# Feed-forward down projection as one level of Strassen's scheme, with one weight sum of each step made by GpSimd

## The reference, cut to what matters

```
D_MODEL = 1024; SEQ = 512; DEPTH = 4; D_FF = 2816

def conv_ffn(x, w_up, conv_w, conv_b, w_down):
    h = x @ w_up                                   # 512 x 1024 times 1024 x 5632
    h = causal_depthwise_conv(h, conv_w) + conv_b  # width 3, each channel by itself
    gate, val = jnp.split(h, 2, axis=-1)
    return (jax.nn.silu(gate) * val) @ w_down      # 512 x 2816 times 2816 x 1024

for i in range(DEPTH):
    ...
    x = x + rms_norm(m, post_mix)
    x = x + rms_norm(conv_ffn(rms_norm(x, pre_ffn), *ffns[i]), post_ffn)
```

## Time and profile before

| | us |
|---|---|
| runs of the kernel before (3) | 2116.58, 2116.76, 2118.89; median 2116.76 |
| profiled execution: span from first to last instruction | 2114.8 |
| profiled execution: another time than its span | none given by the page |
| TensorE matmuls busy, x11988 | 2104.0 |
| DVE busy | 1178.3 |
| ACT busy | 918.0 |
| GpSimd busy | 166.3 |
| HBM traffic | 211.63 MB, mean 100 GB/s |

### The profile page before, as it was taken

The page is one execution under the profiler, slowest core; times in us unless marked ns, Lnnn a source line. Parts: engine busy times, 40 slices in busy tenths (PEclk is TensorE's granted clock), DMA queues, the critical chain, the costliest instruction groups (busy, mean ns, idle before and its releaser), DMA issues.

```text
span 2114.8 us, 32799 instructions
## 1 busy us (share of the span) xinstructions
PE 2104.0 (99%) x11988; PEld 1774.6 (84%) x11988; DVE 1178.3 (56%) x1918; ACT 918.0 (43%) x1527; POOL 166.3 (8%) x190
## 2 busy tenths in 40 slices
PE   9999999999999999999999999999999999999998
PEld 8889888888989888888877898888889889888887
DVE  6665555536366555544697665555446665555534
ACT  5754333325335433333556553334344754333423
POOL 1510000000000000000046300000000520000000
PEclk9999999999999999999999999999999999999999
DMA  7224233331431323333321123333342132333331
GB/s 281 71 90 130 90 98 99 109 136 53 140 130 51 105 94 99 99 109 129 110 77 40 60 77 99 99 99 99 100 139 100 62 101 70 99 99 99 100 99 60
DMA packets 60365, 211.63 MB, mean 100 GB/s; under 512 B 6720, under 2 KB 10944, under 8 KB 59888
## 3 DMA queue, kind: packets, MB, share of 16 engines
q1 hardware_dynamic: 52416, 190.03, 27.4%
q10 hardware_dynamic: 7856, 20.34, 2.7%
HBM read 208.19 MB, written 6.34 MB: 101 GB/s over the span
## 4 chain that ended last, share of the span: by engine, by line
PE 98%; DVE 1%; DMA 0%; ACT 0%; issue 0%; SPq 0%; DVEq 0%; ACTq 0%
PE ps L1545 24%; PE ps L1473 17%; PE ps L1475 17%; PE ps L1474 17%; PE ps L1656 6%; PE ps L1501 2%; PE ps L1503 2%; PE ps L1502 2%; PE ps L1519 1%; PE ps L1518 1%; PE ps L1517 1%; PE ps L1533 1%; PE ps L1819 1%; PE ps L1727 1%; PE ps L1778 1%; PE ps L1701 1%
## 5 line engine op out<-in xcount | busy, mean ns | idle before, releaser
L1473 PE MATMUL ps<-h_hi,w_hi 128*128 128x512 f32 (+1 forms) x1552 | 606.6, 391 | 0.0
L1474 PE MATMUL ps<-h_lo,w_hi 128*128 128x512 f32 (+1 forms) x1552 | 603.2, 389 | 0.0
L1475 PE MATMUL ps<-h_hi,w_lo 128*128 128x512 f32 (+1 forms) x1552 | 603.2, 389 | 0.0
L1427 DVE SCALAR_TENSOR_TENSOR work<-ps,conv_sb,work 128x511 f32<-128x511 f32 (+1 forms) x352 | 247.4, 744 | 437.4 <-ACT work L967 437.1
L1031 DVE TENSOR_TENSOR w_lo<-raw,w_hi 128x1024 fp32r<-128x1024 f32 x312 | 385.8, 1241 | 52.8 <-ACT w_hi L606 43.0
L967 ACT ACTIVATE work<-ps,conv_sb 128x512 f32<-128x512 f32 x176 | 137.2, 779 | 515.2 <-PE ps L1475 486.0
L606 ACT ACTIVATE w_hi<-raw 128x1024 fp32r<-128x1024 f32 x324 | 337.9, 1048 | 34.3 <-PE ps L1545 14.2
L1473 PEld LDWEIGHTS ps<-h_hi,w_hi 128*128 128x128 f32 x1552 | 291.4, 188 | 62.9 <-issue 4.0
L1475 PEld LDWEIGHTS ps<-h_hi,w_lo 128*128 128x128 f32 x1552 | 291.3, 188 | 60.2
L1474 PEld LDWEIGHTS ps<-h_lo,w_hi 128*128 128x128 f32 x1552 | 291.5, 188 | 58.6
L1545 PE MATMUL ps<-w_hi,a_hi 128*128 128x512 f32 x608 | 187.2, 389 | 0.0
(11 more groups left out here) (211 smaller groups left out, 2632.1 us busy)
## 6 DMA issues: line engine op xcount, KB each, us to landing
raw<-slabs SPq DMA_DIRECT2D x324, 512.0 KB, 3.8
bias<-slabs SPq DMA_DIRECT2D x28, 512.0 KB, 6.2
bias_dram<-bias_rows ACTq DMA_DIRECT2D x2, 2048.0 KB, 13.3
g_post<-gains ACTq DMA_DIRECT2D x8, 512.0 KB, 4.2
bias<-bias_dram ACTq DMA_DIRECT2D x2, 2048.0 KB, 9.7
g_pre<-gains ACTq DMA_DIRECT2D x7, 512.0 KB, 5.3
x<-x_in SPq DMA_DIRECT2D x4, 512.0 KB, 7.6
bias<-bias_dram SPq DMA_DIRECT2D x1, 2048.0 KB, 7.7
```

Source lines behind the costliest of these rows:

```text
L1427: ve.scalar_tensor_tensor(y, ps[:, 2 * par + e, 0:SEQ - sh], conv_sb[:, L, t, tap:tap + 1], y, ALU.mult, ALU.add).then_inc(done, 1)
L1473: pe.matmul(ps[:, bank, cols], hi, h_hi[:, k, cols], start=k == 0, stop=False)
L1474: pe.matmul(ps[:, bank, cols], hi, h_lo[:, k, cols], start=False, stop=False)
L1475: last = pe.matmul(ps[:, bank, cols], lo, h_hi[:, k, cols], start=False, stop=k == KT - 1)
```

## The change

One level of Strassen's scheme (Winograd's form) takes the place of the 4 x 2 blocks. Two slabs make a step: the activations of the two slabs, split by token halves, are A11, A12, A21, A22, the slabs' column halves are B11, B12 (even slab) and B21, B22 (odd slab). Seven half products take the place of eight, each for two token tiles of 128 and 512 columns, three matmuls each. All seven are summed over the 11 steps in PSUM before they are combined.

- **Activations, GpSimd** (`down_sums`): five instructions of 256 columns a step (three sums or differences, a copy, another difference), beside the up projection as soon as both gate products of a step are there.
- **Weights, four sums of 512 columns a step**: T1 = B12-B11 on GpSimd (`t1_sum`); T3 = B12-B22 (`sums`), T2 = B11-T3 (`next_sum`), B21-T2 (`last_sum`) on DVE, in place in `raw`. `next_sum` overwrites B12, so it waits for T1. For steps 3 on, T1 is written over activations whose remainder is made, so it waits for `op_lo` of its step.
- **First phase** (P1, P6, P7, P4): 24 matmuls a step, 22 slabs through the ring.
- **Second phase** (P5): 6 matmuls a step, with T1 split into half a ring slot.
- **Third phase** (P2, P3): 12 matmuls a step; the odd slabs are loaded a second time. Tile 0 of the last four steps is done before tile 1.
- DVE combines the products: P1-P7 (`third`), plus P6, plus P4 (`c21`); then P5's sum plus P1 (`c12`), and `c22`. P2 and P3 go on top of what lies in the banks.
- Token tiles 0 and 1 are complete before the third phase, so their norms stand inside it. The early slabs are loaded into `act`, after T1's remainders are made, and split behind the third phase.
- The operand ring: 1024-wide operands for steps in `a_hi`, `h_hi` and their remainders.

The core of the diff (waits on constants and unchanged helpers are left out):

```diff
+            def t1_sum(L, j):
+                even = DOWN[L] + 2 * j
+                b11, b12 = raw[:, raw_slot(even), 0:SEQ], raw[:, raw_slot(even), SEQ:D]
+                pool.wait_ge(raw_in[raw_slot(even)], raw_count(even))
+                if j >= 2:
+                    pool.wait_ge(op_lo, STEPS * L + (j + 1 if j > 2 else 1))
+                pool.tensor_tensor(t1_place(j), b12, b11, ALU.subtract).then_inc(t1_made, 1)
+
+            def down_sums(L):
+                for j in range(STEPS):
+                    if j == STEPS - 1:
+                        for c in range(3):
+                            t1_sum(L, c)
+                    a21, a11, a22, a12 = quarters(j)
+                    s1, kept, s4 = s1_place(j), pa_place(j)[:, 0:HALF], pa_place(j)[:, HALF:SEQ]
+                    pool.wait_ge(gated, FFT * L + 2 * j + 2)
...
+                    pool.tensor_tensor(s1, a21, a22, ALU.add).then_inc(s_made, 1)
+                    pool.tensor_copy(kept, a12).then_inc(s_made, 1)
+                    pool.tensor_tensor(a21, a11, a21, ALU.subtract).then_inc(s_made, 1)
...
+                    pool.tensor_tensor(a12, s1, a11, ALU.subtract).then_inc(s_made, 1)
...
+                    pool.tensor_tensor(s4, kept, a12, ALU.subtract).then_inc(s_made, 1)
+                for j in range(3, STEPS):
+                    t1_sum(L, j)
```

DVE, in the up projection's last pairs and in the down projection:

```diff
+                pair(0, FFT // 2 - 2)
+                pair(1, FFT // 2 - 2)
+                sums(L, 0)
+                next_sum(L, 0)
+                last_sum(L, 0)
                 pair(0, FFT // 2 - 1)
+                sums(L, 1)
+                operand(L, 0)
+                next_sum(L, 1)
+                last_sum(L, 1)
                 pair(1, FFT // 2 - 1)
+                sums(L, 2)
...
+                operand(L, 1)
+                next_sum(L, 2)
+                operand(L, 2)
+                last_sum(L, 2)
+                operand(L, 3)
+                for j in range(3, STEPS):
+                    split_lo(n0 + 2 * j - 2)
+                    sums(L, j)
+                    split_lo(n0 + 2 * j - 1)
+                    next_sum(L, j)
+                    if j + 1 < STEPS:
+                        operand(L, j + 1)
+                    last_sum(L, j)
+                split_lo(n0 + FFT - 2)
+                split_lo(n0 + FFT - 1)
+                t1(0), t1(1), third(0), third(1), t1(2), t1(3), c21(0), c21(1)
+                for j in range(4, STEPS):
+                    t1(j)
+                second(0), second(1), c12(0), c12(1), c22(0), c22(1), second(2), second(3)
+                y(0), add(0), second(4), norm(0), y(1), second(5), add(1), second(6), norm(1)
+                for j in range(7, STEPS):
+                    second(j)
+                lo(0), lo(1), split_early(n), y(2), add(2), split_early(n + 1), norm(2)
+                split_early(n + 2), y(3), add(3), split_early(n + 3), lo(2), norm(3), lo(3)
```

(the calls of one line stand one below the other in the kernel; without the pre-norm the last layer leaves out `norm`, `lo` and the early slabs.) TensorE:

```diff
+                for j in range(1, STEPS - 1):
+                    arrived(j)
+                    p1(j, 0)
+                    p1(j, 1)
+                    p6(j, 0)
+                    p6(j, 1).then_inc(w_used, 1)
+                    odd_arrived(j)
+                    p7(j, 0)
+                    p7(j, 1)
+                    p4(j, 0)
+                    p4(j, 1).then_inc(w_used, 1)
```

```diff
+                ring_slabs(n1 + EARLY, DOWN[L] + FFT)
+                for j in range(STEPS):
+                    if j == RAW and L + 1 < DEPTH:
+                        early_slabs(n2)
+                    ring(second_slot(L, j))
```

More of the change, by code:

```diff
@@ L272, in made, with raw_slot, raw_count, dram @@
         def made(c):
-            return c + 1 - EARLY * passed(c)
+            return c + 1 - EARLY * passed(c) - STEPS * sum(n + FFT + STEPS <= c for n in DOWN)
+        def raw_slot(c):
+            return (made(c) - 1) % RAW
+        def raw_count(c):
+            return 16 * ((made(c) - 1) // RAW + 1)
+        def dram(c):
+            L = max(i for i in range(DEPTH) if BASE[i] <= c)
+            c -= (DOWN_SLOTS - FFT) * L
+            n = DOWN[L] - (DOWN_SLOTS - FFT) * L
+            return n + 2 * (c - n - FFT - STEPS) + 1 if c >= n + FFT else c
+        def summed(c):
+            return any(n <= c < n + FFT for n in DOWN)
         def early_made(c):
@@ L592, in _ @@
                     at_probs(BASE[L])
+                down_sums(L)
         @block.scalar
@@ L716, in norms @@
                         spread_rows(0)
-                if not pre:
-                    last_tile()
             def down(n0, tiles, ready, r0, parts=0, first=False):
@@ L1008, in _ @@
                 if kind == 1:
-                    down(n1, OUT_SLABS, ready, r0, 30 * L + OUT_SLABS)
+                    down(n1, OUT_SLABS, ready, r0, OUT_SLABS * (L + 1))
                 n2 = n1 + OUT_SLABS
@@ L1015, in _ @@
                 ffn_up(L, n2)
-                down(n2 + UP_SLABS, FFT, gated, FFT * L, 30 * (L + 1))
-                norms(2 * L + 2, n2 + UP_SLABS + FFT)
+                ffn_down(L, 2 * L + 2)
                 if L + 1 < DEPTH:
@@ L1030, in split_lo, with norm_steps @@
                 ve.wait_ge(hi_made, 4 * i + made(c))
-                ve.tensor_tensor(w_lo[:, c % RING, :], raw[:, c % RAW, :], w_hi[:, c % RING, :].bitcast(f32),
+                ve.tensor_tensor(w_lo[:, c % RING, :], raw[:, raw_slot(c), :], w_hi[:, c % RING, :].bitcast(f32),
                                  ALU.subtract).then_inc(lo_made, 1)
             def split_early(c):
-                j = c - max(b for b in EARLY_TILES if b <= c)
                 ve.wait_ge(early_hi, early_made(c))
-                ve.tensor_tensor(weight(1, c), early_raw[:, j, :], weight(0, c).bitcast(f32),
+                ve.tensor_tensor(weight(1, c), early_raw(c), weight(0, c).bitcast(f32),
                                  ALU.subtract).then_inc(early_lo, 1)
-            def norms(k, n):
-                post, pre = k > 0, k < 2 * DEPTH
+            def norm_steps(k):
                 p0, q0 = TT * (k - 1), TT * k
@@ L1094, in last_tile, with norms @@
                                                 ALU.mult, ALU.add).then_inc(x_new, 1)
-                if not post:
+                return y, add, norm, lo, last_tile
+            def norms(k, n):
+                y, add, norm, lo, last_tile = norm_steps(k)
+                if k == 0:
                     order = (norm, 0), (norm, 1), (split_lo, n), (lo, 0), (lo, 1), (split_lo, n + 1), (split_lo, n + 2), \
                             (split_lo, n + 3), (norm, 2), (norm, 3), (lo, 2), (lo, 3)
-                elif pre:
+                else:
                     order = (y, 0), (add, 0), (norm, 0), (y, 1), (add, 1), (lo, 0), (norm, 1), \
                             (y, 2), (add, 2), (lo, 1), (norm, 2), (y, 3), (add, 3), (lo, 2), (norm, 3), (lo, 3)
-                else:
-                    order = [(stage, t) for t in range(TT - 1) for stage in (y, add)]
                 for stage, t in order:
                     stage(t)
-                if not pre:
-                    last_tile()
             def down(n0, tiles, a0, first=False):
@@ L1353, in gmlp_in @@
                     if g == 6:
-                        down(n + IN_SLABS[1], OUT_SLABS, 30 * L, first=True)
+                        down(n + IN_SLABS[1], OUT_SLABS, OUT_SLABS * L, first=True)
                 split_lo(n + 14 + AHEAD)
@@ L1443, in ffn_up, with operand, sums @@
+                operand(L, 0)
+                next_sum(L, 1)
+                last_sum(L, 1)
                 pair(1, FFT // 2 - 1)
+                sums(L, 2)
+            def operand(L, j):
+                hi, lo = op_parts(j)
+                ve.wait_ge(op_hi, STEPS * L + j + 1)
+                ve.tensor_tensor(lo, act[:, 2 * j:2 * j + 2, :], hi.bitcast(f32), ALU.subtract).then_inc(op_lo, 1)
+            def sums(L, j):
+                even, odd = DOWN[L] + 2 * j, DOWN[L] + 2 * j + 1
+                b12, b22 = raw[:, raw_slot(even), SEQ:D], raw[:, raw_slot(odd), SEQ:D]
+                ve.wait_ge(raw_in[raw_slot(even)], raw_count(even))
+                ve.wait_ge(raw_in[raw_slot(odd)], raw_count(odd))
+                ve.tensor_tensor(b22, b12, b22, ALU.subtract).then_inc(t_made, 1)
@@ new lines, in next_sum, with last_sum @@
+            def next_sum(L, j):
+                even, odd = DOWN[L] + 2 * j, DOWN[L] + 2 * j + 1
+                b11, b12 = raw[:, raw_slot(even), 0:SEQ], raw[:, raw_slot(even), SEQ:D]
+                t3 = raw[:, raw_slot(odd), SEQ:D]
+                ve.wait_ge(t_made, 3 * (STEPS * L + j) + 1)
+                ve.wait_ge(t1_made, STEPS * L + j + 1)
+                ve.tensor_tensor(b12, b11, t3, ALU.subtract).then_inc(t_made, 1)
+            def last_sum(L, j):
+                even, odd = DOWN[L] + 2 * j, DOWN[L] + 2 * j + 1
+                b21, t2 = raw[:, raw_slot(odd), 0:SEQ], raw[:, raw_slot(even), SEQ:D]
+                ve.wait_ge(t_made, 3 * (STEPS * L + j) + 2)
+                ve.tensor_tensor(b21, b21, t2, ALU.subtract).then_inc(t_made, 1)
```

412 lines of the change are left out of this document (373 added, 39 removed).

## The result

The changed kernel takes 2130.06 us (median; 2126.64 to 2130.91), the kernel before 2116.67 us beside it: ratio 1.0057, 95% interval 1.0045 to 1.0069. It is slower by 0.57%. The profiled span goes from 2114.8 to 2128.4 us, +13.6. That lies inside the range on record (2092 to 2140), but the forecast itself, 2117 and no change, was too low by 13 us, and its own range (2108 to 2126) was missed by 4. One of the nine executions of a kernel further down, the one in which DVE pauses, took 2930.62 us at a granted clock of 0.65; it counts in that kernel's median of 2124.34 us (2123.98 without it), not in its ratio.

The account below looks back on a forecast made before the run. TensorE, busy 99%, bounds the kernel before; DVE was the one to watch. -59.9 + 44.4 (first phase) + 7.3 (third phase) + 7.7 (tail) = -0.5, plus 0.5 for handovers; with 2.0 carried over the 2114.8 span, 2117 us, range 2092 to 2140.

Parts of the forecast that it names:

- the start of phase A: First phase (P1, P6, P7, P4): step 3 ready at 22.3 us, the phase ending 11.1 us late a layer.
- phases B and C: P5, then P2 and P3: nothing late in P5; 2.3 us late a layer after it, last layer 0.4, sum 7.3.
- lower clock: TensorE's clock, left out of the forecast because it was 1.00 in all stretches of the earlier trace; no size or chance.
- Gain, 59.9 us: Down projection: 66 fewer matmuls a layer at 0.2267 us, 15.0 us a layer, if TensorE never waits.
- DVE's step, 5.19 us: First phase: DVE's own work a step, two weight remainders, three sums and the operand's remainder, just below TensorE's 5.44 us.
- GpSimd's sum costs DVE 1.1 us: First phase: B12-B11 on GpSimd takes 1.25 us and excludes DVE for all but 0.15, making the step 6.3 us.
- cheap sum: Rival, first phase: GpSimd's sum costs DVE 0.5 us a step or nothing, giving 2092 or 2079 us; chance 0.21.
- 2.5 us for GpSimd's five: Start of the first phase: GpSimd's five 256-column instructions of the last step delay DVE 2.5 us; step 2 ready at 14.9.
- a rival at 22 us: First phase: loads into `raw` landing at 5.3 us make DVE's step 7.1, 22 us more, 2139; chance 0.17.
- the rival of dearer norms: Third phase: norms between the slabs cost 2.5 us more in each of three layers, 2125 us; chance 0.12.
- The tail, 7.7 us: Behind the third phase: DVE's early remainders between norms of tiles 2 and 3 delay transposes, 2.0 + 3.7 + 2.0 us.

Follow-up runs that it names:

- The best version: Changed kernel with B12-B11 of steps 3 to 10 on DVE before each step's first sum, operand 1 split earlier, early remainders moved up: 2101.42 us, ratio 0.9925.

## Why the prediction was right and where it failed

The large terms of the sum are right. What it lacks is spread over four places: some 8 us at the start of phase A, 2 from late loads, 2 in phases B and C, and 1.6 from TensorE's lower clock in one tail.

- **Gain, 59.9 us**: right; 11988 - 11724 = 264 matmuls, at 0.227 us wherever TensorE is fed.
- **DVE's step, 5.19 us**: right. The best version has 5.81 with one more sum of 0.60.
- **GpSimd's sum costs DVE 1.1 us**: right, by the rows, by leaving it out and by doubling it. The rival "cheap sum" is refuted.
- **The start of phase A, 2.5 us for GpSimd's five**: this step failed. It let the engines take turns, because the two places it had the earlier trace rows were of one instruction each. In fact GpSimd got no turn for 9.7 us, and DVE then stood idle for 4.5 us behind all that had piled up on GpSimd. Step 3 is ready 24.2 to 24.3 us into the stage in all four layers and not 22.3, and as the steps behind it are DVE's 6.3 us, nothing makes up for it: TensorE gets step 9's slab at 62.2 us in layer 0, forecast 60.1. That is some 2 us a layer, 8 of the 12 us by which the stages were off. That turns would have come out near the forecast is shown by the run with the pause, and that the queue behind the shut-out makes the loss by the run with the sum on DVE.
- **The rest of the stages, some 4 us**: about half of it late loads. DVE waited 5.0 us for `raw` in 8 places, and only part of that moved a step: TensorE gets step 9's slab at 62.6 us in layer 2 and 62.9 in layer 3, where the longest of these waits (1.34 us) is. Loads in layer 0's phase A land in 3.1 / 3.8 / 5.3 us (minimum, median, maximum), close to the earlier trace rows. The prediction had this as a rival at 22 us. How the late loads come about was not tested.
- **Phases B and C**: the wait before step 5 is 1.8 us, forecast 1.9, and its cause is DVE's whole work, as forecast; the rival of dearer norms (2.5 us more a layer) did not come. From the end of phase A the stage takes 49.4 us in layer 0, forecast 49.0; 0.4 to 0.8 too much a layer, some 2 in all.
- **The tail, 7.7 us**: 9.4. The numbers are right in layers 0 and 2 (2.1 each, forecast 2.0), and in layer 1 too where the clock stays up (26.1 against 22.5 before is 3.6, forecast 3.7); with the clock down it is 5.2. But the waits were not the ones named, so this is partly luck. In layer 0 TensorE waits once, 1.7 us for the second early remainder, and not for the norm of tile 2; in layer 1 it waits for that remainder and for h, where the forecast had h alone.
- **The lower clock**: wrongly left out. The mean granted clock fell from 0.999 to 0.994: six stretches, some 20 us in all, at the lower level, in which TensorE did some 10 us less of work. Five lie in phase A, where they cost next to nothing, because DVE decides when the next step begins. The layers show it: where the clock fell behind step 1 (layers 0 to 2), TensorE waits 2.9 to 3.05 us before step 3, where it did not (layer 3) 4.5, and step 3 begins 24.2 to 24.3 us into the stage in all four. The sixth lies in the tail of layer 1, where TensorE is the one that is waited for, and costs 1.6 us, nearly all by which the tails were off.

What stays open is what lets GpSimd in. In every run that left it work there, it was shut out behind the convolution taps of the last pair until DVE paused once (for a wait, or for 0.1 us before a dependent instruction). After such a pause it won the next boundary nearly each time, although DVE ran back to back again. In the steady steps a sum that is issued 0.23 us into a DVE instruction gets in behind it. In the run with the five on DVE one issued 0.22 us into another (414.10) did not, and at its step 7 (446.98) one issued 0.23 us into the same instruction as in the steady steps was passed too, until DVE waited. Neither the form of the instruction nor its moment nor its neighbours on DVE explain it alone.

## What to carry to other kernels

When DVE is to run back to back on two-input instructions, work on GpSimd is not parallel work: each of its instructions costs DVE about its own length, here 1.1 us where DVE itself would need 0.6, and an instruction that DVE waits for later may not get in at all until DVE stops. Place what GpSimd must deliver where DVE idles anyway, or give DVE the work, and keep an instruction off the place right behind the one that it reads. Before pricing a step by one engine's load, list who queues behind whom on the other engine, since one shut-out delays all of it; and before moving a norm, see which transposes and remainders follow it. A lower clock behind a new wait costs only where TensorE, and not the engine that feeds it, decides when the next piece begins: here nothing to speak of in phase A, 1.6 us in a tail.

## What was not expected of the hardware

- A GpSimd instruction that is ready first can lose to nine DVE instructions in a row (9.7 us for 0.73 of work), also a copy with one input (9.41).
- A pause of DVE of about 0.1 us ends it (2.26 us in all), and turns are taken from there, with the exception above (446.98).
- Of eight idles of 2.9 to 4.5 us on TensorE five had a stretch at the 1.2 GHz level (seven matmuls 0.43 us apart behind the first), idles of 0.8 us none; behind the same idle of 1.8 us the clock fell in four kernels of nine.
- A DVE instruction right behind the one it depends on starts 0.10 to 0.19 us later than an independent one (0.72 and 0.79 for 0.60).
